# Rounds of two matmuls instead of four in the decay products of 16 gated heads, with keys and queries of both token blocks gathered by ScalarE

## The chip, the core and the metric

The kernel runs on one core of a Trainium2 chip. The time is what the device takes for one execution, in microseconds (us). PE is TensorE (PEld its weight loads), ACT is ScalarE, DVE is VectorE, POOL is GpSimd, SP issues DMAs. A bank is one of the eight accumulators that PE writes and ACT or DVE read.

## The reference, cut to what matters

Two transformer layers' worth of blocks run on 256 tokens of width 2048: a gated MLP, a hybrid mixer (dilated attention and gated linear attention), a cross attention over 256 memory tokens, a second MLP, then a recurrent block (RG-LRU and a gated recurrence with 16 heads) and a differential attention. The change is about the 16 heads:

```python
def hgrn2_chunkwise(q, k, v, log_f):
    ...
    def step(state, inp):
        qc, kc, vc, gc = inp
        b = jnp.cumsum(gc, axis=2)
        o_inter = jnp.einsum('bhtk,bhkv->bhtv', qc * jnp.exp(b), state)
        decay = jnp.exp(jnp.where(mask, b[:, :, :, None, :] - b[:, :, None, :, :], -jnp.inf))
        scores = jnp.einsum('bhtk,bhsk,bhtsk->bhts', qc, kc, decay)
        o = o_inter + jnp.einsum('bhts,bhsv->bhtv', scores, vc)
    ...
```

For each head (128 keys, 128 values) the score of query t and key s is their product times a decay by the product of all forget gates between them. The kernel computes the whole lower triangle of the 256 x 256 scores, without chunks and without a state.

## The kernel before

**Weights.** The kernel is a row of stages by name: up1a to dn1c (first MLP), mixa, gla, wout, memk, xq, memv, xo (cross attention), up2a to dn2c, rg, rouA, hg, rouB, att, aout. Every stage streams weights in units of 512 KB, one at a time through a ring of RING = 4 slots: SP loads `w_raw`, ACT rounds it to `w_high` (L1053), DVE makes the rest `w_low` (L1533), PE multiplies both (L553 to L556, or L593 to L595 for token-major units of 12 matmuls). ACT and DVE run LEAD = 3 units ahead of PE. A split waits until PE has finished the unit that used its slot.

**Banks.** A unit accumulates in one of the two banks of `gemm`; DVE takes a bank out (L1565, L2085) before PE may start it again (`evacuated`, L554).

**hg.** Eight iterations (`each`, `heads_phase`) of 16 units, with two heads in each. The table `AT_H` says at which unit of the iteration which step of the heads stands, on all engines alike: `(step, 0)` belongs to this iteration's heads, `(step, 1)` to those of the iteration before. PE does a step ahead of the unit with that number.

**Decay products.** The scores come by levels. At level s a token range of 2^s tokens is a half: queries in an odd half meet keys in the even half to their left. Tiles: `B` holds the keys of both heads (`B[:, 2:4, :]`, 256 tokens), `C` the queries, `Dm` the gates; all three are parts of `work`. PE (`decay`, L784) multiplies keys and queries of each token block of 128 (2 heads x 2 blocks = 4 matmuls of 128 x 128) into a bank (`p_a` and `p_b` in turn). DVE (L1817) copies from it what the mask of this level picks (`level_masks`) into `scores_t` (`ST[:, head, 0 or 1 or 2, :]`: 0 and 2 the two diagonal blocks, 1 the block between them). POOL (L2284, L2295, L2296, L2299) scales the odd queries and the even keys by the gates' products of the level for the next round. Step 0 needs no gate; step 7 is the last within a block (L781, 64 x 64), step 8 the block between the two (L772). Semaphores: PE's `round` lets POOL scale and DVE copy; POOL's `started` (first product) lets round 1 go, its `updated` the later rounds; DVE's `placed` gives a bank back. "mix" (L747, L748) multiplies the scores with the values, "oturn" (L754) transposes.

**rouA1** takes its banks by `lead` (two of them) and **memv** runs the cross attention's steps inside its eight units: PE scores (L931) at unit 2, DVE `largest`, ACT `power` (L1363), DVE `weigh` (L1986), PE `turn` (L943), ACT `copy_probs` (L1369), two heads at a time at units 2 to 6, then L990 multiplies with the values (L2031).

## Time and profile before

| | us |
|---|---|
| time, median of 3 runs | 3301.19 (3300.79 to 3301.6) |
| the profiled execution | 3301.96 |
| its span in the profile | 3300.2 |
| PE busy | 3267.8 (99%) |
| DVE busy | 2222.7 (67%) |
| ACT busy | 1720.4 (52%) |
| POOL busy | 367.3 (11%) |

The profile is of one execution. Busy times are sums over an engine's rows. In a timeline each row is one group of like instructions that follow one another: start, duration, line, what it writes and reads, how many; in brackets the idle time of the engine ahead of it and whose work ended that. A matmul in full float32 leaves two records, so that four matmuls are a row of x8. A matmul row's duration holds the drain of its last matmul, over which the next work already runs: what a row costs is the distance to the next one.

### The profile page before, as it was taken

What the parts mean: (1) busy time and instruction counts of PE and PEld (TensorE: products, weight loads), DVE (VectorE), ACT (ScalarE), POOL (GpSimd) and SP (SyncE); (2) the same over time, 40 slices, a digit from 0 to 9 for tenths busy, and PEclk for the clock granted to TensorE, in tenths of its full rate; (3) what the DMA queues carried; (4) which work ended last, traced back from release to release, by engine and by line L of the source; (5) the groups of instructions that cost most, each with busy time, mean ns of one, the idle gap of its engine ahead of it and who ended that gap; (6) DMA issues with size and microseconds to landing.
All of it is one profiled execution on the core that took longest, in us unless ns stands there. A gap on an engine that the chain in (4) does not pass through costs nothing.

```text
span 3300.2 us, 54641 instructions
## 1 busy us (share of the span) xinstructions
PE 3267.8 (99%) x17950; PEld 2811.3 (85%) x17950; DVE 2222.7 (67%) x3262; ACT 1720.4 (52%) x2555; POOL 367.3 (11%) x378
## 2 busy tenths in 40 slices
PE   8999999999999999999999999999999999999999
PEld 7888888887888878888888888888888888888888
DVE  7666666677655867666676677887556567666566
ACT  5444444455555655444444456764444445555554
POOL 1000000011000301000000001220333341100000
PEclk9999999999999999999999999999999999999999
DMA  6666566555555655656666656556555555555555
GB/s 228 188 198 186 186 193 186 188 180 165 172 170 175 200 156 176 190 188 185 192 186 186 190 177 198 184 173 187 158 153 159 154 157 173 185 169 180 172 172 165
DMA packets 280057, 592.46 MB, mean 180 GB/s; under 512 B 19856, under 2 KB 171664, under 8 KB 279840
## 3 DMA queue, kind: packets, MB, share of 16 engines
q1 hardware_dynamic: 278816, 587.12, 57.1%
q10 hardware_dynamic: 1152, 4.19, 0.3%
q8 instruction: 51, 0.84, 0.1%
q14 instruction: 38, 0.31, 0.0%
HBM read 589.14 MB, written 2.10 MB: 179 GB/s over the span
## 4 chain that ended last, share of the span: by engine, by line
PE 90%; issue 4%; DVE 4%; ACT 1%; POOL 0%; DMA 0%; SPq 0%; POOLq 0%; ACTq 0%; DVEq 0%
PE bank L554 41%; PE bank L553 10%; PE bank L556 10%; PE bank L593 7%; PE bank L595 7%; PE bank L594 7%; PE bank L784 2%; DVE w_low L1533 2%; PE bank L796 1%; DVE normed L1578 1%; ACT w_high L1053 1%; POOL work L2296 0%; PE bank L748 0%; PE bank L678 0%; DMA w_raw<-w_up1a 0%
## 5 line engine op out<-in xcount | busy, mean ns | idle before, releaser
L1533 DVE TENSOR_TENSOR w_low<-w_raw,w_high 128x1024 fp32r<-128x1024 f32 (+1 forms) x1120 | 1374.5, 1236 | 637.9 <-ACT w_high L1053 619.1
L1053 ACT ACTIVATE w_high<-w_raw 128x1024 fp32r<-128x1024 f32 (+1 forms) x1120 | 1166.4, 1044 | 765.0 <-PE bank L595 408.5
L554 PE MATMUL bank<-normed,w_high 128*128 128x512 f32 x3968 | 1263.4, 397 | 12.0 <-DVE w_low L1533 9.9
L554 PE MATMUL bank<-mixed,w_high 128*128 128x512 f32 x2432 | 771.3, 397 | 5.2 <-DVE increment L1565 4.3
L554 PEld LDWEIGHTS bank<-normed,w_high 128*128 128x128 f32 x3968 | 609.7, 189 | 13.6 <-issue 9.9
L553 PE MATMUL bank<-normed,w_low 128*128 128x256 f32 x1984 | 552.8, 279 | 0.0
L556 PE MATMUL bank<-normed,w_low 128*128 128x256 f32 x1984 | 550.9, 278 | 0.0
L593 PE MATMUL bank<-w_high,normed 128*128 128x512 f32 x1152 | 462.9, 402 | 1.1 <-DVE w_low L1533 1.1
L553 PEld LDWEIGHTS bank<-normed,w_low 128*128 128x128 f32 x1984 | 373.0, 188 | 90.8
L595 PE MATMUL bank<-w_high,normed 128*128 128x512 f32 x1152 | 450.0, 391 | 0.0
L594 PE MATMUL bank<-w_low,normed 128*128 128x512 f32 x1152 | 449.3, 390 | 0.0
L556 PEld LDWEIGHTS bank<-normed,w_low 128*128 128x128 f32 x1984 | 373.7, 188 | 83.8
L1073 ACT ACTIVATE parts<-bank 128x256 f32<-128x256 f32 x376 | 144.5, 384 | 575.5 <-PE bank L554 575.3
L554 PEld LDWEIGHTS bank<-mixed,w_high 128*128 128x128 f32 x2432 | 373.0, 189 | 7.5 <-DVE w_low L1533 3.8
L553 PE MATMUL bank<-mixed,w_low 128*128 128x256 f32 x1216 | 338.9, 279 | 0.0
L556 PE MATMUL bank<-mixed,w_low 128*128 128x256 f32 x1216 | 337.6, 278 | 0.0
L553 PEld LDWEIGHTS bank<-mixed,w_low 128*128 128x128 f32 x1216 | 228.6, 188 | 55.6
L556 PEld LDWEIGHTS bank<-mixed,w_low 128*128 128x128 f32 x1216 | 229.0, 188 | 51.8
L595 PEld LDWEIGHTS bank<-w_high,normed 128*128 128x128 f32 x1152 | 216.5, 188 | 46.4
L593 PEld LDWEIGHTS bank<-w_high,normed 128*128 128x128 f32 x1152 | 217.0, 188 | 42.9 <-issue 1.7
L594 PEld LDWEIGHTS bank<-w_low,normed 128*128 128x128 f32 x1152 | 217.1, 188 | 41.9
L1556 DVE TENSOR_TENSOR increment<-bank,parts 128x256 f32<-128x256 f32 x244 | 103.5, 424 | 214.9 <-ACT parts L1073 214.9
(312 smaller groups left out, 2275.5 us busy)
## 6 DMA issues: line engine op xcount, KB each, us to landing
w_raw<-w_att SPq DMA_DIRECT2D x128, 512.0 KB, 3.9
w_raw<-w_up1a SPq DMA_DIRECT2D x64, 512.0 KB, 4.2
w_raw<-w_up1b SPq DMA_DIRECT2D x64, 512.0 KB, 4.1
w_raw<-w_up2a SPq DMA_DIRECT2D x64, 512.0 KB, 4.1
w_raw<-w_up2b SPq DMA_DIRECT2D x64, 512.0 KB, 3.9
w_raw<-w_rg SPq DMA_DIRECT2D x64, 512.0 KB, 4.2
w_raw<-w_hg SPq DMA_DIRECT2D x64, 512.0 KB, 3.6
w_raw<-w_hg SPq DMA_DIRECT2D x128, 256.0 KB, 2.8
```

What stands on the lines that cost most here:

```text
L553: nc.tensor.matmul(banks[b][:, 0:S], lo, x[:, 0:S], start=False, stop=False)
L554: last = nc.tensor.matmul(banks[b][:, :], hi, x, start=starts and k == 0, stop=stop)
L556: last = nc.tensor.matmul(banks[b][:, 0:S], lo, x[:, 0:S], start=False, stop=False)
L593: nc.tensor.matmul(banks[b][:, :], x_hi, hi, start=starts and k == 0, stop=False)
L594: nc.tensor.matmul(banks[b][:, :], x_hi, lo, start=False, stop=False)
L595: last = nc.tensor.matmul(banks[b][:, :], x_lo, hi, start=False, stop=stops and k == UT // 4 - 1)
L784: last = nc.tensor.matmul(b_out[:, c * P:(c + 1) * P], B[:, 2 + hd, b * P:(b + 1) * P], rhs[:, hd, b * P:(b + 1) * P], start=True, stop=True)
L796: last = nc.tensor.matmul(b_out[:, n * S:(n + 1) * S], gw[:, t * P:(t + 1) * P], C[:, k, :], start=k == 0, stop=k == 1)
L1053: A_(wh[slot][:, 0:width], raw[slot][:, 0:width], ACT.Copy).then_inc(wh_done, 1)
L1073: A_(parts[b], banks[b][:, S:2 * S], ACT.Copy).then_inc(part_ready, 1)
L1533: TT(wl[slot][:, 0:width], raw[slot][:, 0:width], wh[slot][:, 0:width].bitcast(F32), ALU.subtract).then_inc(wl_done, 1)
L1556: TT(inc[:, b, :], gemm[b][:, 0:S], part[b], ALU.add).then_inc(evacuated, 1)
```

## The change

- In hg, rounds 1 to 7 have two matmuls, one for each head (L801 after). Their weights are the new tile `held` (a part of `gate_weights`): in each place the keys of token block 0 in even halves, the queries of block 1 in odd halves. Their moving side is `passed`: the keys of block 1 and the queries of block 0 read in place in `work`. One product then holds block 0's scores as keys by queries, and block 1's as queries by keys.
- ACT fills `held` ahead of each of these rounds with two copies (L1246, L1247), which wait for POOL's `started` or `updated`. PE waits for ACT's new `held`.
- DVE picks with two masked copies of 128 x 2 x 64, and block 1's scores land the other way round. The new step 9 (at unit 2 of the next iteration) transposes them: two PE transposes (L786) and one DVE copy to `turned`. The mix waits for that.
- The masks for the other orientation are made once, in up2b (six PE transposes) between DVE copies in dn2a and dn2b; POOL clears a part of `scores_t` at the start of rg.
- POOL's products and their order in hg stay as they are.
- rouA1 uses four banks in turn. In memv DVE's `largest` and ACT's `power` stand for all four heads at unit 2, `weigh` for all at unit 3; `turn` and `copy_probs` of heads 0 and 1 at unit 5, of heads 2 and 3 behind the last unit. In up1a ACT's four partial sums of squares move from units 0 to 2 to units 1 to 4, one each.

Line numbers of the changed kernel are higher than before: L784 is L801 or L813, L593 to L595 are L609 to L611, L1053 is L1093.

ACT in hg, units 8 to 15 of one iteration: from the last preparation of the gates over the splits beside rounds 1 to 5. `mixed` is the store of the heads before.

```order
L1232 ACTIVATE work<-work 128x512
...
L1053 ACTIVATE w_high<-w_raw 128x1024
...
L1217 ACTIVATE mixed<-bank,vectors 128x2x256
...
L1053 ACTIVATE w_high<-w_raw 128x1024
...
L1053 ACTIVATE w_high<-w_raw 128x1024 x2
...
L1053 ACTIVATE w_high<-w_raw 128x1024
```

```order
L1093 ACTIVATE w_high<-w_raw 128x1024
...
L1268 ACTIVATE mixed<-bank,vectors 128x2x256
...
L1093 ACTIVATE w_high<-w_raw 128x1024
...
L1246 ACTIVATE gate_weights<-work 128x2x64
L1247 ACTIVATE gate_weights<-work 128x2x64
...
L1246 ACTIVATE gate_weights<-work 128x2x32x2
L1247 ACTIVATE gate_weights<-work 128x2x32x2
...
L1093 ACTIVATE w_high<-w_raw 128x1024
...
L1246 ACTIVATE gate_weights<-work 128x2x16x4
L1247 ACTIVATE gate_weights<-work 128x2x16x4
```

In the first piece ACT has nothing but splits beside the rounds. In the second a pair of copies stands ahead of each round, two pairs (for rounds 1 and 2) behind the split of unit 13, and the next splits behind the pairs.

PE in hg, around rounds 0 to 2. `work` are keys and queries, `normed` the tokens of the unit.

```order
L595 MATMUL bank<-w_high,normed 128x512
...
L784 MATMUL bank<-work 128x128 x8
...
L593 MATMUL bank<-w_high,normed 128x512
L594 MATMUL bank<-w_low,normed 128x512
...
L595 MATMUL bank<-w_high,normed 128x512
...
L784 MATMUL bank<-work 128x128 x4
```

```order
L611 MATMUL bank<-w_high,normed 128x512
...
L813 MATMUL bank<-work 128x128 x4
...
L801 MATMUL bank<-work,gate_weights 128x128 x2
...
L609 MATMUL bank<-w_high,normed 128x512
L610 MATMUL bank<-w_low,normed 128x512
...
L611 MATMUL bank<-w_high,normed 128x512
...
L801 MATMUL bank<-work,gate_weights 128x128 x2
```

Before, rounds 0 and 1 are one piece of eight matmuls. After, round 1 has its own wait (for ACT's copies, `gate_weights`) right behind round 0, ahead of the unit.

ACT in memv, from the splits behind the gains of the cross attention's queries on: L1363 and L1414 are the exponentials, L1369 and L1420 the copies of the turned probabilities.

```order
L1053 ACTIVATE w_high<-w_raw 128x1024 x2
L1363 ACT_TABLE_LOAD
L1363 ACTIVATE work,softmax_stats<-bank,softmax_stats,q_rstd 128x256 x4
L1053 ACTIVATE w_high<-w_raw 128x1024
L1363 ACTIVATE work,softmax_stats<-bank,softmax_stats,q_rstd 128x256 x4
L1053 ACTIVATE w_high<-w_raw 128x1024
L1369 ACTIVATE gate_weights<-bank 128x512 x2
L1053 ACTIVATE w_high<-w_raw 128x1024
L1369 ACTIVATE block_products<-bank 128x512
L1369 ACTIVATE probs_t<-bank 128x512
L1053 ACTIVATE w_high<-w_raw 128x1024
L1412 ACTIVATE mem_values<-bank,mem_rstd 128x4x128
```

```order
L1093 ACTIVATE w_high<-w_raw 128x1024
L1414 ACT_TABLE_LOAD
L1414 ACTIVATE work,softmax_stats<-bank,softmax_stats,q_rstd 128x256 x8
L1093 ACTIVATE w_high<-w_raw 128x1024 x3
L1420 ACTIVATE gate_weights<-bank 128x512 x2
L1093 ACTIVATE w_high<-w_raw 128x1024 x2
L1463 ACTIVATE mem_values<-bank,mem_rstd 128x4x128
L1420 ACTIVATE block_products<-bank 128x512
L1420 ACTIVATE probs_t<-bank 128x512
```

All eight exponentials now stand together ahead of three splits, and the copies of heads 2 and 3 (`block_products`, `probs_t`) behind the last split and the values.

```diff
                 10: [("oturn", 1)], 11: [("store", 1), (0, 0)]}
-        AT_H = {0: [("values", 1), (7, 1)], 1: [(8, 1)], 3: [("mix", 1)], 4: [("norm", 1)], 5: [("gate", 1)], 7: [("oturn", 1)],
+        AT_H = {0: [("values", 1), (7, 1)], 1: [(8, 1)], 2: [(9, 1)], 3: [("mix", 1)], 4: [("norm", 1)], 5: [("gate", 1)], 7: [("oturn", 1)],
                 8: [("prepare", 0)], 9: [("store", 1)], 10: [(0, 0), (1, 0)]}
...
+            if name == "rouA1" and j // 2 % 2:
+                return p_t, p_o
             return (p_b, p_o) if name == "aout1" and j < 2 else gemm
...
             return (it - HEADS_G) * 16 + (place["hg"][0] * RING + 16)
+
+        def pieces(offset, step, h):
+
+            pair = work[:, :, :].rearrange("p n s -> p (n s)")[:, offset:offset + 2 * (step + h)]
+            return pair.rearrange("p (e r) -> p e r", e=2)[:, :, 0:P].rearrange("p e (n u t) -> p e n u t", u=2, t=h)[:, :, :, 0, :]
+
+        def passed(hd, step):
+
+            return pieces((6 + hd) * S + P, S + P, 1 << (step - 1))
...
         def _(pe):
-            def unit(qq, slot, parts, src, banks=gemm, later=None):
+            def unit(qq, slot, parts, src, banks=gemm, later=None, depth=2):
...
                 for b, k0, nk, starts, stops, grp in parts:
-                    if starts and not (isinstance(grp, int) and grp < len(banks)):
-
-                        pe.wait_ge(evacuated, grp - (len(banks) - 1))
+                    if starts and not (isinstance(grp, int) and grp < depth):
+
+                        pe.wait_ge(evacuated, grp - (depth - 1))
                     for k in range(nk):
...
                 if step == "mix":
-                    pe.wait_ge(dec["placed"], rounds(it, heads) + (3 if heads == 1 else 9))
+                    pe.wait_ge(dec["placed"], rounds(it, heads) + (3 if heads == 1 else 10))
                     pe.wait_ge(rec["valued"], it + 1)
...
                             nc.tensor.matmul(to, ST[:, n, 1, :], V_D[:, 0, cols], start=True, stop=False)
-                        last = nc.tensor.matmul(to, ST[:, n, 2 * b, :], V_D[:, b, cols], start=b == 0, stop=True)
+                        own_block = ST[:, n, 2 * b, :] if heads == 1 else turned[:, n, :] if b else ST[:, n, 2, :]
+                        last = nc.tensor.matmul(to, own_block, V_D[:, b, cols], start=b == 0, stop=True)
                     last.then_inc(rec["mixed"], 1)
...
                         pe.wait_ge(dec["placed"], rounds(it, 1) + (step - 6))
+                    if step == 9:
+                        pe.wait_ge(dec["placed"], rounds(it, 2) + 8)
+                        for hd in range(2):
+                            last = nc.tensor.transpose(b_out[:, hd * P:(hd + 1) * P], ST[:, hd, 0, :], C_("ident"))
+                        last.then_inc(dec["round"], 1)
+                        return
+                    if heads == 2 and 1 <= step <= 7:
+                        pe.wait_ge(dec["held"], keeps(it) + step)
                     if heads == 2 and step >= 2:
...
                             continue
-                        rhs = B if step == 0 and heads == 2 else C
+                        if heads == 2 and step:
+                            last = nc.tensor.matmul(b_out[:, hd * P:(hd + 1) * P], held[:, hd, :], passed(hd, step),
+                                                    start=True, stop=True)
+                            continue
+                        rhs = B if heads == 2 else C
                         for b in range(NB):
-                            c = 2 * hd + b
+                            c = 2 * hd + (b if heads == 1 else 1 - b)
                             if step == LEVELS - 1:
...
                             score(hd)
-                    if j in (5, 6):
-                        turn(2 * j - 10)
-                        turn(2 * j - 9)
+                    if j == 5:
+                        turn(0)
+                        turn(1)
                     unit_tokens(q0 + j // RING, j % RING, 2 * j, XN, mem_banks, j == 0, j == 7)
+                turn(2)
+                turn(3)
                 pe.wait_ge(mem["valued"], 2)
...
             for name in names:
+                if name == "up2b":
+                    pe.wait_ge(dec["spread"], 1)
+                    flat = C[:, :, :].rearrange("p n s -> p (n s)")
+                    for step in range(6):
+                        last = nc.tensor.transpose((p_a, p_b)[step // 4][:, step % 4 * P:(step % 4 + 1) * P],
+                                                   flat[:, step * P:(step + 1) * P], C_("ident"))
+                    last.then_inc(dec["faced"], 1)
                 if name.startswith("up"):
...
                     prepare(it, grp, heads, it)
+                if heads == 2 and isinstance(step, int) and step < 7:
+                    h = 1 << step
+                    if step == 0:
+                        act.wait_ge(dec["started"], it + 1)
+                    else:
+                        act.wait_ge(dec["updated"], updates(it, 2) + step)
+                    to = held.rearrange("p h (n u t) -> p h n u t", u=2, t=h)
+                    keys = B[:, 2:4, 0:P].rearrange("p h (n u t) -> p h n u t", u=2, t=h)
+                    queries = C[:, 0:2, P:S].rearrange("p h (n u t) -> p h n u t", u=2, t=h)
+                    A_(to[:, :, :, 0, :], keys[:, :, :, 0, :], ACT.Copy)
+                    A_(to[:, :, :, 1, :], queries[:, :, :, 1, :], ACT.Copy).then_inc(dec["held"], 1)
                 if step == "values":
...
                                scale=cross_gain[:, 0:1]).then_inc(crs["gained"], 1)
-                    if j in (3, 4):
-                        power(2 * j - 6)
-                        power(2 * j - 5)
-                    if j in (5, 6):
-                        copy_probs(2 * j - 10)
-                        copy_probs(2 * j - 9)
+                    if j == 2:
+                        for hd in range(HEADS_X):
+                            power(hd)
+                    if j == 5:
+                        copy_probs(0)
+                        copy_probs(1)
                 act.wait_ge(pe_unit, place["xo"][0] * RING)
...
                    scale=rstd_m[:, 1:2]).then_inc(mem["valued"], 1)
+                copy_probs(2)
+                copy_probs(3)
                 for hd in range(HEADS_X):
...
                         dve.wait_ge(dec["placed"], rounds(it, heads) + at)
+                    if heads == 2 and step == 0:
+                        dve.wait_ge(dec["cleared"], 1)
                     if not isinstance(it, int):
...
                             "p (h s) -> p h s", h=heads)).then_inc(dec["placed"], 1)
+                    elif step == 9:
+                        nc.vector.tensor_copy(turned, b_in[:, 0:2 * P].rearrange(
+                            "p (h s) -> p h s", h=2)).then_inc(dec["placed"], 1)
+                    elif step == LEVELS - 1 and heads == 2:
+                        x = b_in[:, 0:2 * P].rearrange("p (h e t) -> p h e t", h=2, e=2)
+                        nc.vector.tensor_copy(ST[P // 2:P, :, 0, 0:P // 2], x[P // 2:P, :, 0, :])
+                        nc.vector.tensor_copy(ST[0:P // 2, :, 2, P // 2:P], x[0:P // 2, :, 1, :]).then_inc(dec["placed"], 1)
+                    elif heads == 2 and step:
+                        h = 1 << (step - 1)
+                        x = b_in[:, 0:2 * P].rearrange("p (h e n t) -> p h e n t", h=2, e=2, t=h)
+                        for e in range(2):
+                            last = nc.vector.copy_predicated(
+                                ST[:, :, 2 * e, :].rearrange("p h (n u t) -> p h n u t", u=2, t=h)[:, :, :, e, :],
+                                level_mask[:, step, :].rearrange("p (n u t) -> p n u t", u=2, t=h)[:, :, e, :].unsqueeze(1
+                                ).broadcast_to([P, 2, P // (2 * h), h]),
+                                x[:, :, e, :, :])
+                        last.then_inc(dec["placed"], 1)
                     elif step == LEVELS - 1:
...
                     if j in (2, 3):
-                        largest(2 * j - 4)
-                        largest(2 * j - 3)
-                    if j in (4, 5):
-                        weigh(2 * j - 8)
-                        weigh(2 * j - 7)
+                        for hd in range(HEADS_X):
+                            (largest, weigh)[j - 2](hd)
                 dve.wait_ge(rms["rooted"], NORMED["memk"] + 1)
...
                 PT_(C[:, 0:heads, :], B[:, 0:heads, :], Dm[:, 0:heads, :], ALU.mult).then_inc(dec["started"], 1)
-                total, at = Dm[:, 0:heads, :].rearrange("p h s -> p (h s)"), 0
+                total, at = Dm[:, 0:2, :].rearrange("p h s -> p (h s)"), 0
                 for level in range(LEVELS - 1):
                     half = 1 << level
-                    n = heads * S // (2 * half)
-                    qv = C[:, 0:heads, :].rearrange("p h (n e t) -> p (h n) e t", e=2, t=half)
-                    kv = B[:, 2:2 + heads, :].rearrange("p h (n e t) -> p (h n) e t", e=2, t=half)
+                    n = S // half
+                    all_q = C[:, 0:2, :].rearrange("p h (n e t) -> p (h n) e t", e=2, t=half)
+                    all_k = B[:, 2:4, :].rearrange("p h (n e t) -> p (h n) e t", e=2, t=half)
                     tv = total.rearrange("p (n e) -> p n e", e=2)
-
-                    pool.wait_ge(dec["round"], rounds(it, heads) + (level + 2))
-                    own.settle()
-                    PT_(qv[:, :, 1, :], qv[:, :, 1, :], tv[:, :, 0:1].broadcast_to([P, n, half]), ALU.mult)
-                    PT_(kv[:, :, 0, :], kv[:, :, 0, :], tv[:, :, 1:2].broadcast_to([P, n, half]),
+                    pool.wait_ge(dec["round"], rounds(it, 2) + (level + 2))
+                    own.settle()
+                    PT_(all_q[:, :, 1, :], all_q[:, :, 1, :], tv[:, :, 0:1].broadcast_to([P, n, half]), ALU.mult)
+                    PT_(all_k[:, :, 0, :], all_k[:, :, 0, :], tv[:, :, 1:2].broadcast_to([P, n, half]),
                         ALU.mult).then_inc(dec["updated"], 1)
```

## Rows read from the trace of the kernel before

**Rows 1.** The page, part 1: busy us, share and instructions of each engine

```profile
PE 3267.8 (99%) x17950; PEld 2811.3 (85%) x17950; DVE 2222.7 (67%) x3262; ACT 1720.4 (52%) x2555; POOL 367.3 (11%) x378
```

**Rows 2.** PE's waits: line, what it waited for, us in total, times, longest

```profile
PE bank L554 <- DVE increment L1565: 4.3, 6, 1.8
...
PE bank L554 <- DVE work L2085: 1.4, 1, 1.4
...
PE bank L990 <- DVE mem_values L2031: 0.9, 1, 0.9
```

**Rows 3.** Busy time by stretch: us, PE, PEld, DVE, ACT, POOL, PEclk, DMA

```profile
2308.00:2740.00 432.00, 430.06 (x2458) 368.55 (x2457) 261.07 (x367) 202.17 (x298) 158.38 (x175) 1.00 0.50 156
1200.00:1220.00 20.00, 17.69 (x76) 14.42 (x76) 12.93 (x27) 12.14 (x26) 1.64 (x1) 0.92 0.38 118
2226.00:2230.00 4.00, 3.99 (x16) 3.48 (x17) 3.36 (x5) 0.00 (x0) 0.00 (x0) 0.64 0.23 88
25.00:29.00 4.00, 3.82 (x22) 3.36 (x23) 4.00 (x4) 1.16 (x2) 3.78 (x3) 1.00 0.82 256
```

**Rows 4.** Timeline of PE, one iteration: start, us, line, operation, [idle before]

```profile
2434.02 1.95 PE L784 MATMUL bank<-work 128*128 128x128 f32 x16
...
2438.91 1.15 PE L784 MATMUL bank<-work 128*128 128x128 f32 x8 [0.19 <-POOL work L2296]
...
2446.30 1.06 PE L784 MATMUL bank<-work 128*128 128x128 f32 x8
...
2449.94 1.05 PE L784 MATMUL bank<-work 128*128 128x128 f32 x8
...
2457.33 0.68 PE L781 MATMUL bank<-work 128*64 128x64 f32 x8
...
2460.83 0.60 PE L772 MATMUL bank<-work 128*128 128x128 f32 x4
...
2466.85 0.60 PE L748 MATMUL bank<-v_raw_and_tokens,scores_t 128*128 128x128 f32 x4
...
2479.34 0.60 PE L754 MATMUL bank<-constants,head_out 128*128 128x128 f32 x4
```

**Rows 5.** Timeline of POOL, the same iteration

```profile
2433.43 1.29 POOL L2284 TENSOR_TENSOR work<-work 128x512 f32<-128x512 f32 x1 [12.41 <-ACT work L1232]
...
2440.22 1.46 POOL L2295 TENSOR_TENSOR work<-work,block_products 128x256 f32<-128x256 f32 x1 [0.86 <-PE bank L784]
2441.64 0.75 POOL L2296 TENSOR_TENSOR work<-work,block_products 128x256 f32<-128x256 f32 x1
...
2447.53 0.65 POOL L2295 TENSOR_TENSOR work<-work,block_products 128x256 f32<-128x256 f32 x1 [1.12 <-PE bank L784]
2448.13 1.63 POOL L2296 TENSOR_TENSOR work<-work,block_products 128x256 f32<-128x256 f32 x1
```

**Rows 6.** ACT: timeline in gla and hg, and the group of L1149

```profile
933.06 0.40 ACT L1234 ACTIVATE work<-work 128x256 f32<-128x256 f32 x1
933.37 0.40 ACT L1235 ACTIVATE work<-work 128x256 f32<-128x256 f32 x1
...
2434.78 1.05 ACT L1053 ACTIVATE w_high<-w_raw 128x1024 fp32r<-128x1024 f32 x1
...
L1149 ACT ACTIVATE work<-work,root_qk 128x128 f32<-128x128 f32 x48 | 16.0, 389 | 3.9 <-POOL root_qk L2251 3.9
```

**Rows 7.** Timeline of DVE, the same iteration

```profile
2439.84 1.23 DVE L1533 TENSOR_TENSOR w_low<-w_raw,w_high 128x1024 fp32r<-128x1024 f32 x1 [0.16 <-ACT w_high L1053]
...
2447.59 1.66 DVE L1533 TENSOR_TENSOR w_low<-w_raw,w_high 128x1024 fp32r<-128x1024 f32 x1 [1.28 <-ACT w_high L1053]
...
2465.71 1.22 DVE L1533 TENSOR_TENSOR w_low<-w_raw,w_high 128x1024 fp32r<-128x1024 f32 x1
```

**Rows 8.** Timeline of PE in memv and in rouA1

```profile
1216.49 1.84 PE L943 MATMUL bank<-constants,work 128*128 128x128 f32 x8 [2.31 <-DVE work L1986]
...
2226.01 0.47 PE L554 MATMUL bank<-mixed,w_high 128*128 128x512 f32 x1 [1.81 <-DVE increment L1565]
```

31 lines of the change are left out of this document (25 added, 6 removed).

## The prediction

> **What bounds the kernel now.** I read the page's busy line first: PE is busy for 3267.8 of 3300.2 us [rows 1]. So the time is PE's work plus some 32 us in which PE waits, and an edit counts only if it changes PE's own instructions, or a wait of PE. The view of PE's waits names those [rows 2]: the longest is for the first split at the start, which the change does not touch; the others are small and single, and rows 2 keeps the three that the change aims at. The table by stage comes next [rows 3]: the decay phase (2308 to 2740 us, eight iterations of 54 us, all of it at full clock) has PE busy for 430.06 of 432.00 us. There is nothing to win there from waits, only from PE instructions, and much to lose if a new wait appears. The rounds of one iteration in the timelines of PE and POOL [rows 4, 5] show how close that is. PE starts a round at 2446.30 and the next at 2449.94, 3.65 us later: 2.74 us of unit work (12 matmuls 0.23 us apart, as they follow one another in PE's timeline) and 0.90 us for the round. Beside it runs a chain: the round ends (2447.36), POOL starts 0.17 us later (2447.53) and ends at 2449.76, and PE's next round starts at 2449.94. The chain is 0.1 to 0.2 us shorter than PE's own period. PE bounds the rounds, by a hair, and POOL is next.
>
> **The sum is made against the profiled run, 3301.96 us** (span 3300.2), 0.77 us above the median of 3301.19; I take that off at the end.
>
> **The rounds.** A round of steps 1 to 6 has four matmuls before and two after. Half of 0.90 is 0.45 for two matmuls of this size. Such two stand in the trace as step 8 (a row of 4 records, 0.60 us long, of which the last matmul's drain lies under the next work) [rows 4]. So a round costs PE 0.45 us less, and PE alone would have a period of 3.20 us. But the chain gains a link: POOL's products, then two ACT copies, then PE. Each copy has 128 elements a partition. No such copy stands in the trace. The 256-wide copies are 0.40 us each, the second starting 0.31 after the first, the 1024-wide split 1.057 [rows 6]. The slope between them, 0.85 ns an element, gives 0.29 for one and 0.50 us for the pair. The nearest 128-wide row is L1149 with 389 ns, which has a scale per row; two of those are 0.69. I take 0.50, because the copies have no scale, and keep 0.69 for the range. The two new hand-overs I take as 0.04 (POOL to ACT) and 0.10 us (ACT to PE), estimates below the 0.17 that PE to POOL takes in this round; at 0.17 each the chain would be 0.2 longer.
>
> The chain after: round 0.60 (the row of 4 records) + 0.17 + POOL 2.23 (2447.53 to 2449.76) + 0.04 + 0.50 + 0.10 = **3.64 us**. It replaces PE's 3.65. What PE saves in a round is what it then waits: about 0.45 us idle before each round. The term that can move is POOL's 2.23. Alone its two products are 0.65 and 0.75; the other 0.8 is DVE's split, which stretches whichever product it meets (L2296 1.63 us at 2448.13 while the DVE split is 1.66; L2295 1.46 us at 2440.22) [rows 5, 7]. DVE's split follows ACT's split, which follows the end of the unit ahead of the round. If PE idles 0.45 us before the round, the split comes 0.45 earlier against the round, at +0.85 instead of +1.29, and POOL starts at +0.77. That is on the edge. If the split wins, both products stand behind it: at 2440.22 the level ended 1.32 us after the split's end. A level is then at most 1.23 + 1.32 = 2.55. I take 3.70 for the period, between 3.64 and 3.96.
>
> **Round 1** is where time is lost for certain. Rounds 0 and 1 stand back to back before (the x16 row at 2434.02, round 1 at about 2434.93). Now round 1 needs the copies, which need POOL's first product (2433.43 + 1.29 = 2434.72), and on ACT's queue they stand behind the split of 2434.78, which ends at 2435.83 [rows 5, 6]. Copies until 2436.33, round 1 at about 2436.4: PE idles some 1.4 us. It saves 0.47 of that by two matmuls less. Then POOL starts at 2437.15 with DVE's split already running, as at 2440.22, where the level took 2.17; with the split further on than there it takes 1.8 to 2.1 and ends at about 2439.1. With 0.64 for copies and hand-overs round 2 starts at 2439.7 where it was 2438.91: +0.8. Behind the waiting copies on ACT stands the next split. It starts 0.8 us later than now, and since PE uses a split three units later (8 us), nobody waits for it.
>
> Rounds 2 to 7: five periods of 3.70 for 18.42 us before, +0.1. Step 7 was four small matmuls for some 0.6 us (the row of 0.68) and is two for 0.45: -0.15. The new step 9 has two transposes at 0.11 (four at 2479.34, 0.60 with the drain, 0.44 without): +0.22 [rows 4]. Its copy on DVE stands behind a split that ends at 2466.93 [rows 7] and takes about 0.42, with the mix at 2466.85 now waiting for it; both shift together by 0.9, so PE waits some 0.4 us there. Sum: 0.8 + 0.1 - 0.15 + 0.22 + 0.4 = **+1.4 us an iteration, +11 for eight**. With the chain at 3.64, a level as short after round 1 as the first figure says and no wait at the mix it is +0.5, so +4; with 3.85 it is +2.3, so +19.
>
> DVE's mask copies get shorter and are on no path. POOL's memset and the masks' copies in dn2a and dn2b stand beside PE work in stages where PE waits for nothing, with splits three units ahead, 8 us: nothing. The six transposes in up2b are PE work: 6 x 0.11 = +0.7.
>
> **The other waits.** rouA1: DVE's take of an accumulated bank comes late behind the scan and PE stands for 1.81 us at 2226.01 [rows 8]; with four banks it need not wait. After the stop the granted clock is 0.64 over the next 4 us [rows 3]: most of that stretch ran at 1.2 GHz and not 2.4, and 4 x 0.36 = 1.4 us were lost. With 0.4 us of the other waits on this take (six make 4.3 [rows 2]), -3.6. memv: PE stands 2.31 us for the weighing at 1216.49 [rows 8]; the weighing moves from units 4 and 5 to unit 3 and the exponentials to unit 2. The eight of L1363 are 4.4 us in a row on ACT and the splits behind them come later, but the turns are needed only at unit 5, 8.2 us on. The clock is 0.92 in those 20 us: 1.6 us more. Also 0.9 us for the values (L990) [rows 2], which two moved turns now cover. Together -4.8. If the later splits make PE wait instead, -3. Start: PE waits 1.4 us (L554 on DVE's L2085) [rows 2] for a take that stands behind two DVE splits; the squares move off ACT's way and the splits come about one ACT operation earlier: -1.4, between -0.5 and -1.6. Sum of the side edits: -3.6 - 4.8 - 1.4 + 0.7 = **-9.1**, between -6 and -11.
>
> **Total**: 3301.96 + 11.2 - 9.1 = 3304.1, minus 0.77: **3303 us**. No change that a measurement can tell: some 0.2% (6.6 us) is what it can.
>
> **The rivals.**
> A, PE bounds the rounds. If the DVE split fell outside POOL's two products, a level would be 1.40 and the chain 2.81, and the period would be PE's 3.20. An iteration gets 0.8 - 5 x 0.49 - 0.15 + 0.22 + 0.4 = -1.2 us, eight -10, total 3301.2 - 10 - 9.1 = 3282. Against it: PE, ACT and DVE follow one another so that the split starts at +0.85 to +1.29 and POOL works from +0.77 to +2.2; every level in the trace meets it. Chance 0.12.
> B, slower: the clock falls. PE idles about 1.4 us ahead of round 1, eight times. It fell after idle times of 1.81 and 2.31 us [rows 8]; it did not after the 1.4 at the start [rows 2], where the clock is 1.00 over the next 4 us [rows 3]. It decides from somewhere between these. Then each iteration loses up to 1.6 us, less the 0.45 of one round's slack: 8 x 1.2 = +10, total 3313. Chance 0.13.
> C, slower: the chain is longer than priced, by the split going ahead of POOL (2.55), the pair at 0.69 and 0.15 to PE: up to 0.60 + 0.17 + 2.55 + 0.04 + 0.69 + 0.15 = 4.20. Every 0.1 us above 3.65 costs 5 x 8 x 0.1 = 4 us; at 3.95 it is +12 over my sum with 1 more at round 2, total 3315; at 4.20 3325. It decides from 3.85 on (by which the total passes 3308). For it: POOL's 1.46 us product, which shows that order [rows 5]. Against: only then is PE idle long enough that the split leads, and the two orders hold each other near 3.75. Chance 0.13.
> The Trainium skill ("SBUF — State Buffer", section "Who interferes with whom") says that issue order decides who blocks: the engine that comes first to the shared pair holds it for the whole instruction. By that rule the product behind the split of 2447.59 to 2449.25 would need its whole 0.75 us after it; the row ends 0.51 after. By the rule the chain would be 3.88 and the time about 3310, near rival C; by the row it is 3.64, and the trace decides.
> D, the side edits do not give what I took (another wait takes the place of the one removed, as the splits behind eight exponentials would in memv): -6 instead of -9.1, 3306. It lies in my forecast's range.
>
> **Chances.** Forecast with D 0.62, A 0.12, B 0.13, C 0.13. The range 3290 to 3315 leaves out A (0.12) and half of C and a tail of B, together about 0.2. Faster by over 0.2% (below 3294.6): A and the lowest part of the forecast, 0.18. Slower (above 3307.8): B, C and the forecast's upper end, 0.3. Same: 0.52.
>
> **What the profile after would show.** PE rows of two matmuls, about 0.44 of PE time each, 3.7 us apart, each with an idle of 0.4 to 0.5 before it, released by ACT; ahead of round 1 an idle of 1.2 to 1.5. Some 33 to 38 us of new PE waits on the copies in all (8 x (1.4 + 6 x 0.45 + 0.4) = 36). POOL products of 2.2 us in sum a level. ACT pairs of 0.5. No PE wait over 1 us in rouA1 and memv and the clock at 1.00 there. Window 2308 to 2740 grown by some 11 us. I am wrong if the period is 3.2 or above 3.85, if the clock drops in the decay phase, or if an iteration waits elsewhere.

## The result and the profile after

| | before | after |
|---|---|---|
| time, median of 8 runs, us | 3301.97 | 3312.59 |
| span of the profiled execution, us | 3300.2 | 3310.5 |
| PE busy, us | 3267.8 | 3256.6 |

The changed kernel is slower: the ratio is 1.0033, with a 95% interval of 1.0024 to 1.0043. One of its eight executions took 3402.81 us at a granted clock of 0.916, and the ratio leaves it out. The forecast was 3303 us, in a range of 3290 to 3315.

The page, part 1, of the changed kernel (compare [rows 1]), and under it its PE waits (compare [rows 2]):

```profile
PE 3256.6 (98%) x17748; PEld 2788.6 (84%) x17748; DVE 2206.1 (67%) x3285; ACT 1745.5 (53%) x2667; POOL 363.9 (11%) x379
```

```profile
PE bank L801 <- ACT gate_weights L1247: 27.1, 53, 1.2
PE bank L570 <- DVE w_low L1586: 12.1, 2, 10.2
PE bank L570 <- DVE increment L1618: 2.1, 4, 1.1
...
PE bank L765 <- DVE gate_weights L1866: 1.1, 7, 0.2
```

PE has 11 us less work and 22 us more idle time. One new wait, for ACT's copies, makes 27.1 us (53 times), and some of the old ones are gone. The waits of [rows 2] for L1565 have gone from 4.3 to 2.1 us, those for L2085 and for the values (L990) are gone, and so is the one of [rows 8] in memv.

Where the 10.3 us come from can be read off landmarks: PE instructions that wait for the same thing in both kernels, and so mark the same point of the program. First of the kernel before, then of the changed one (PE timeline; start, duration, line, idle before):

```profile
40.62 0.70 PE L643 MATMUL bank<-diag,ones 128*128 128x256 f32 x2 [0.36 <-DVE diag L1652]
...
1198.69 1.06 PE L950 MATMUL bank<-constants,work 128*128 128x128 f32 x8 [0.44 <-DVE work L2020]
...
1264.13 0.61 PE L622 MATMUL bank<-ones,squares_sum 128*128 128x1 f32 x4 [0.28 <-DVE normed L1578]
...
1715.21 0.50 PE L554 MATMUL bank<-mixed,w_high 128*128 128x512 f32 x1 [0.86 <-DVE w_low L1533]
...
2325.60 1.16 PE L784 MATMUL bank<-work 128*128 128x128 f32 x8 [0.38 <-ACT work L1232]
```

```profile
39.46 0.70 PE L659 MATMUL bank<-diag,ones 128*128 128x256 f32 x2 [0.38 <-DVE diag L1705]
...
1197.53 1.07 PE L980 MATMUL bank<-constants,work 128*128 128x128 f32 x8 [0.44 <-DVE work L2092]
...
1257.86 0.61 PE L638 MATMUL bank<-ones,squares_sum 128*128 128x1 f32 x4 [0.27 <-DVE normed L1631]
...
1710.62 0.50 PE L570 MATMUL bank<-mixed,w_high 128*128 128x512 f32 x1 [1.88 <-DVE w_low L1586]
...
2316.61 1.16 PE L813 MATMUL bank<-work 128*128 128x128 f32 x8 [0.38 <-ACT work L1283]
```

The differences after minus before are -1.16 us at the first two (the start), -6.27 at the third, -4.59 at the fourth and -8.99 at round 0 of hg. So the start gave 1.2 us, memv 5.1, and rouA1 4.4; between the third and the fourth, where the masks are turned, 1.7 were lost. The start is the least certain of these: its landmark lies between 38.09 and 39.46 us in the profiles of the changed kernel and of the experiments below that have its new start, and at 40.62 and 40.96 in the two with the old one, so that the gain there is 1.2 to 2.9 us by the execution. In that place stood:

```profile
1708.31 0.87 DVE L2214 CAST level_masks<-bank 128x64 int32<-128x64 f32 x6
1709.34 3.50 DVE L1586 TENSOR_TENSOR w_low<-w_raw,w_high 128x1024 fp32r<-128x1024 f32 x3 [0.16 <-DVE level_masks L2214]
```

Six casts of the turned masks stand ahead of three queued splits on DVE, 1.03 us from the first cast to the splits, and PE's wait at the fourth landmark is 1.88 instead of 0.86.

The granted clock is full again where it was 0.92 and 0.64 in [rows 3] (windows of the changed kernel, columns as there):

```profile
1200.00:1220.00 20.00, 20.00 (x94) 16.78 (x94) 13.27 (x28) 12.61 (x26) 1.64 (x1) 1.00 0.37 128
2226.00:2240.00 14.00, 14.00 (x83) 12.22 (x82) 11.77 (x19) 6.68 (x10) 0.00 (x0) 1.00 0.75 234
```

So 9.0 us are won ahead of hg, and all of it and 9.7 more are lost in it (0.6 more behind it). One iteration of the changed kernel (PE timeline, compare [rows 4]):

```profile
2428.56 1.06 PE L813 MATMUL bank<-work 128*128 128x128 f32 x8
2430.82 0.72 PE L801 MATMUL bank<-work,gate_weights 128*128 128x128 f32 x4 [1.21 <-ACT gate_weights L1247]
...
2434.43 0.72 PE L801 MATMUL bank<-work,gate_weights 128*128 128x128 f32 x4 [0.15 <-issue]
...
2438.54 0.71 PE L801 MATMUL bank<-work,gate_weights 128*128 128x128 f32 x4 [0.64 <-ACT gate_weights L1247]
...
2446.32 0.71 PE L801 MATMUL bank<-work,gate_weights 128*128 128x128 f32 x4 [0.42 <-ACT gate_weights L1247]
...
2450.12 0.71 PE L801 MATMUL bank<-work,gate_weights 128*128 128x128 f32 x4 [0.34 <-ACT gate_weights L1247]
...
2453.96 0.71 PE L801 MATMUL bank<-work,gate_weights 128*128 128x128 f32 x4 [0.37 <-ACT gate_weights L1247]
...
2463.87 0.71 PE L765 MATMUL bank<-v_raw_and_tokens,scores_t 128*128 128x128 f32 x4 [0.15 <-DVE gate_weights L1866]
```

Measured from round 0 (2434.02 before, 2428.56 after), round 2 is at 5.87 us instead of 4.89, round 7 at 25.40 instead of 23.31, and the mix at 35.31 instead of 32.83. An iteration is 56.6 us instead of 54.0. What sets the period shows beside the rounds of 2446.32 and 2450.12 on POOL, ACT and DVE (compare [rows 5, 6, 7]):

```profile
2447.19 1.58 POOL L2376 TENSOR_TENSOR work<-work,block_products 128x256 f32<-128x256 f32 x1 [1.46 <-PE bank L801]
2448.72 0.63 POOL L2377 TENSOR_TENSOR work<-work,block_products 128x256 f32<-128x256 f32 x1
```

```profile
2449.39 0.31 ACT L1246 ACTIVATE gate_weights<-work 128x128 f32<-128x128 f32 x1 [2.38 <-POOL work L2377]
2449.61 0.29 ACT L1247 ACTIVATE gate_weights<-work 128x128 f32<-128x128 f32 x1
```

```profile
2447.05 1.23 DVE L1586 TENSOR_TENSOR w_low<-w_raw,w_high 128x1024 fp32r<-128x1024 f32 x1 [2.23 <-ACT w_high L1093]
```

The chain reads: round 0.71, to POOL 0.16, POOL 2.16 (2447.19 to 2449.35), to ACT 0.04, the pair 0.51 (2449.39 to 2449.90), to PE 0.22. That is 3.80 us, the distance of the two rounds. DVE's split now starts 0.14 us ahead of POOL, and POOL's first product is the long one (1.58), not the second as in [rows 5].

The 4.11 us between the rounds of 2434.43 and 2438.54 have the same links but a longer one on POOL:

```profile
2435.32 0.74 POOL L2376 TENSOR_TENSOR work<-work,block_products 128x256 f32<-128x256 f32 x1 [1.10 <-PE bank L801]
2436.02 1.73 POOL L2377 TENSOR_TENSOR work<-work,block_products 128x256 f32<-128x256 f32 x1
```

That level takes 2.43 us (2435.32 to 2437.75). POOL was first there, by 0.09 us, and the product that met nothing took 0.74 and not 0.63. The four levels after it take 2.26, 2.22, 2.16 and 2.20.

PE's idle times understate what the chain costs. Where nothing makes PE wait its rounds come 3.19 us apart (dve_after_pool below), so it stands for some 0.6 us of these 3.80, of which the profile counts 0.34 as idle: the drain of the matmul ahead of the wait and the longer round behind it count as busy.

### The profile page after: what moved, and what is told of

It reads as the page before. It is cut to its first block, busy times and chain, and to the rows that moved or that the text cites. A ratio compares the mean times of both kernels' runs of the same rounds, so it can differ in the third digit from the quotient of the medians.

```text
span 3310.5 us, 54497 instructions
## 1 busy us (share of the span) xinstructions
PE 3256.6 (98%) x17748; PEld 2788.6 (84%) x17748; DVE 2206.1 (67%) x3285; ACT 1745.5 (53%) x2667; POOL 363.9 (11%) x379
## 4 chain that ended last, share of the span: by engine, by line
PE 87%; issue 4%; DVE 4%; ACT 3%; POOL 2%; DMA 0%; ACTq 0%; POOLq 0%; SPq 0%; DVEq 0%
PE bank L570 43%; PE bank L569 11%; PE bank L572 11%; PE bank L609 6%; PE bank L611 6%; PE bank L610 6%; ACT w_high L1093 1%; DVE w_low L1586 1%; PE bank L801 1%; POOL work L2377 1%; PE bank L825 1%; DVE normed L1631 1%; ACT gate_weights L1247 0%; PE bank L765 0%; PE bank L694 0%
## 5 line engine op out<-in xcount | busy, mean ns | idle before, releaser
L1093 ACT ACTIVATE w_high<-w_raw 128x1024 fp32r<-128x1024 f32 (+1 forms) x1120 | 1166.0, 1044 | 630.9 <-PE bank L570 347.8
L570 PE MATMUL bank<-normed,w_high 128*128 128x512 f32 x3968 | 1265.0, 397 | 10.9 <-DVE w_low L1586 10.2
L570 PEld LDWEIGHTS bank<-normed,w_high 128*128 128x128 f32 x3968 | 610.3, 189 | 11.7 <-issue 10.2
L609 PE MATMUL bank<-w_high,normed 128*128 128x512 f32 x1152 | 462.4, 401 | 1.1 <-DVE w_low L1586 1.1
L611 PE MATMUL bank<-w_high,normed 128*128 128x512 f32 x1152 | 449.7, 390 | 0.0
L611 PEld LDWEIGHTS bank<-w_high,normed 128*128 128x128 f32 x1152 | 216.2, 188 | 46.4
L609 PEld LDWEIGHTS bank<-w_high,normed 128*128 128x128 f32 x1152 | 216.6, 188 | 42.9 <-issue 1.7
```

The costliest lines, as they stand in the source:

```text
L570: last = nc.tensor.matmul(banks[b][:, :], hi, x, start=starts and k == 0, stop=stop)
L609: nc.tensor.matmul(banks[b][:, :], x_hi, hi, start=starts and k == 0, stop=False)
L611: last = nc.tensor.matmul(banks[b][:, :], x_lo, hi, start=False, stop=stops and k == UT // 4 - 1)
L1093: A_(wh[slot][:, 0:width], raw[slot][:, 0:width], ACT.Copy).then_inc(wh_done, 1)
```

## The experiments

The twelve kernels ran in three groups of four, each beside the kernel before, whose median was 3301.34 (sides_only, decay_only, dve_after_pool, copy_more), 3301.8 (held_wait_last, first_pair_early, dve_after_pool_from_2, from_2_and_pair) and 3302.77 us (the other four). Ratios are to it. Where a difference is between kernels of different groups, or to the changed kernel with its 3312.59 us, it is uncertain by this 1 to 1.5 us. Line numbers shift by a few between the kernels.

Two things ahead of hg differ from profile to profile and have nothing to do with the edits in it: the start, as said, and whether the clock falls behind a wait of 1.9 us in dn2a (see the masks below; 1.8 us). The time from round 0 of hg's first iteration to the end of the span is free of both; it can still hold up to some 2 us of slow clock in the last 40 us:

| kernel | us |
|---|---|
| before | 974.6 |
| changed | 993.9 |
| sides_only | 974.9 |
| decay_only | 993.5 |
| dve_after_pool | 977.6 |
| dve_after_pool_from_2 | 966.1 |
| old_rounds_dve_after_pool | 974.5 |
| copy_more | 1003.3 |
| held_wait_last | 987.0 |
| first_pair_early | 992.2 |
| from_2_and_pair | 964.9 |
| split_between | 956.0 |
| masks_later | 993.6 |
| split_between_masks_later | 956.3 |

**The parts alone.** The edit of the first is to leave the decay part out, of the second to leave the edits of rouA1, memv and up1a out; the diff of both is a part of the one shown with the change.

> The kernel before with the edits outside the decay products alone: four banks in rouA1, the moved steps of memv, the moved squares of up1a; no mirrored masks, rounds of four matmuls. My theory (the side edits and the decay part add up, each read off the trace by the shift of landmarks): -1.2 at the start, -5.1 in memv, -4.4 in rouA1, so 10.7 us less than the kernel before, 3291 us. A rival by which the gains were only shifted waits that come back later in the kernel: less than 6 us gained, 3296 or more.

Measured: 3291.16 us, ratio 0.9968 (0.9956 to 0.998): -10.2.

> The changed kernel with those three side edits undone: rounds of two matmuls, the masks mirrored in dn2a to dn2b, step 9. Theory: the decay phase costs +18.7 and the masks +1.7 by the landmarks of the two traces, so 21 us above the kernel before, 3323 us. If the slower decay phase and the faster side edits were tied to one another (the phase starts 9 us earlier in the changed kernel), it would be off that by 3 us or more.

Measured: 3322.18 us, ratio 1.0062 (1.0048 to 1.0076): +20.8. The two add up to +10.6, which is what the change does. Within the noise the parts are independent, and the landmarks told their sizes (-10.7 and +21 expected).

**POOL and DVE apart.** DVE waits ahead of its split until POOL's products of the level are done:

```diff
+                        if name == "hg" and 10 <= j <= 15:
+                            dve.wait_ge(dec["updated"], updates(i + HEADS_G, 2) + (j - 9))
+                            if not isinstance(i, int):
+                                dve.sem_inc(dve_passed, 1)
                         ahead(name, qq, j, nb, last)
```

> The changed kernel; DVE's split beside each of rounds 1 to 6 waits until POOL's two products of that level are done (one wait more on DVE, nothing else). Theory: what makes the period 3.85 us is the meeting of POOL's products with DVE's split; apart, a level is 1.35 us, the chain 3.0, and PE bounds the rounds at 3.20 to 3.25 us. Five periods 0.6 shorter and round 2 0.4 earlier, 8 iterations: 27 us less than the changed kernel, 3285 us, with POOL's products at 0.65 and 0.65. Rival 1: the two copies on ACT and their hand-overs bound the period by themselves; then the products get shorter but the period stays above 3.6, 3305 or more. Rival 2: the splits now come too late for PE and waits on w_low take the gain: over 3 us of such waits in the decay phase.

Measured: 3296.22 us, ratio 0.9983 (0.9974 to 0.9992): 16 us less than the changed kernel, where 27 were expected. Its PE timeline in one iteration, then POOL beside the round of 2440.05, and DVE:

```profile
2433.53 0.72 PE L801 MATMUL bank<-work,gate_weights 128*128 128x128 f32 x4 [1.57 <-DVE scores_t L1889]
...
2436.84 0.61 PE L801 MATMUL bank<-work,gate_weights 128*128 128x128 f32 x4
...
2440.05 0.61 PE L801 MATMUL bank<-work,gate_weights 128*128 128x128 f32 x4
```

```profile
2440.82 0.65 POOL L2380 TENSOR_TENSOR work<-work,block_products 128x256 f32<-128x256 f32 x1 [1.65 <-PE bank L801]
2441.43 0.65 POOL L2381 TENSOR_TENSOR work<-work,block_products 128x256 f32<-128x256 f32 x1
```

```profile
2432.64 0.76 DVE L1889 COPY_PREDICATED scores_t<-level_masks,bank 128x256 f32<-128x256 int32 x2
...
2442.32 1.23 DVE L1586 TENSOR_TENSOR w_low<-w_raw,w_high 128x1024 fp32r<-128x1024 f32 x1 [1.54 <-POOL work L2381]
```

POOL's products are 0.65 each and rounds 3 to 7 come 3.19 to 3.21 us apart with no idle time: PE bounds them. Rival 1 falls, and no wait on w_low appeared, so rival 2 falls too. The missing 11 us are at round 2, where PE waits 1.57 us for DVE's masked copy of round 0 (2432.64), which stands behind the split that now waits: seven such waits, 10.9 us in all.

Without the wait beside round 1:

```diff
-                        if name == "hg" and 10 <= j <= 15:
+                        if name == "hg" and 11 <= j <= 15:
```

> As dve_after_pool, without the wait at round 1 (so beside rounds 2 to 6 only). There rounds 3 to 7 came 3.19 us apart, but round 2 waited 1.57 us for DVE's masked copies of round 0, which stood behind the delayed split. Theory: round 2 is where the changed kernel has it and the five periods are 3.2: 8 x 3.6 = 29 us less than the changed kernel, 3284 us. If the delayed splits cost something of their own, it is over 3288.

Measured: 3284.62 us, ratio 0.9947 (0.9934 to 0.9961), 28 us less than the changed kernel, where the theory had 29.

**The old rounds with the same wait.** The same edit on the kernel of sides_only:

> The kernel of sides_only (rounds of four matmuls) with the wait of dve_after_pool_from_2 on DVE. Theory: there PE itself bounds the rounds at 3.65 us, so shorter POOL levels give nothing but the 0.1 us before round 2 that they never had: within 1.5 us of sides_only, 3291. Rival: the old rounds were bound by the same meeting of POOL and DVE; then they gain as the new ones did, 10 us or more.

Measured: 3290.44 us, ratio 0.9962 (0.9948 to 0.9976). The median is 0.7 us below that of sides_only, but its group ran 1.4 us slower; from round 0 of hg to the end the two differ by 0.4 us. POOL beside the round of 2434.90 in it:

```profile
2436.12 0.65 POOL L2303 TENSOR_TENSOR work<-work,block_products 128x256 f32<-128x256 f32 x1 [2.09 <-PE bank L786]
2436.73 0.65 POOL L2304 TENSOR_TENSOR work<-work,block_products 128x256 f32<-128x256 f32 x1
```

The level is 1.26 us, one microsecond shorter than the 2.24 in sides_only, and the rounds come 3.65 us apart all the same. So the old rounds are bound by PE, and the rival falls: with four matmuls the chain is shorter by ACT's link and PE's own period longer, and the meeting of POOL and DVE costs nothing. Only with the change does it come onto the path.

**The link on ACT.** One copy more ahead of each pair:

```diff
+                    spare = FD[:, 2:4, P:S].rearrange("p h (n u t) -> p h n u t", u=2, t=h)
+                    A_(spare[:, :, :, 0, :], keys[:, :, :, 0, :], ACT.Copy)
                     A_(to[:, :, :, 0, :], keys[:, :, :, 0, :], ACT.Copy)
```

> The changed kernel with one copy more on ACT (the same keys once more, into a part of the tile that nothing reads, 0.21 us to the next) ahead of each pair. Theory: POOL, ACT's pair, PE's round are one loop with nothing beside it that gives; +0.2 us for each of seven rounds, eight iterations: +12 us on the changed kernel, 3324. Rival: the meeting with DVE's split sets the period, and a later round lets the split get further ahead of POOL, so that POOL's level shrinks by what ACT adds: +4 us or less, 3316.

Measured: 3322.27 us, ratio 1.0063 (1.0049 to 1.0077): +9.7 on the changed kernel (+9.4 from round 0 of hg on), nearer the theory's 12 than the rival's 4. Rounds 3 to 7 come 4.0 to 4.1 us apart. The link is on the path for four fifths of its length.

**The order of PE's waits.** In rounds 2 to 7 of the changed kernel PE waits for ACT's `held` first, then for `placed` and `updated`. The edit puts `held` last:

```diff
-                    if heads == 2 and 1 <= step <= 7:
-                        pe.wait_ge(dec["held"], keeps(it) + step)
                     if heads == 2 and step >= 2:

                         pe.wait_ge(dec["placed"], rounds(it, 2) + (step - 1))
                         pe.wait_ge(dec["updated"], updates(it, 2) + (step - 1))
+                    if heads == 2 and 1 <= step <= 7:
+                        pe.wait_ge(dec["held"], keeps(it) + step)
```

> The changed kernel; PE waits for ACT's copies behind its other two waits of the round, not ahead of them. In the changed kernel PE starts 0.05 us after the copies where it has this wait alone (round 1) and 0.22 us after them where two more, long fulfilled, stand behind it (rounds 2 to 7). Theory 1: those two cost 0.17 us on the path; without them 6 x 8 x 0.12 to 0.17, 6 to 8 us less, 3305. Theory 2: POOL's first product waits for the end of DVE's split anyway in rounds 3 to 7, whenever the round ends, so that an earlier round gains nothing in most of them: 2 us less or nothing, 3311.

Measured: 3305.86 us, ratio 1.0011 (1.0002 to 1.002), 6.7 us less than the changed kernel (6.9 from round 0 of hg on): theory 1. One round of it on PE, ACT, POOL and DVE:

```profile
2445.32 0.71 PE L801 MATMUL bank<-work,gate_weights 128*128 128x128 f32 x4 [0.24 <-ACT gate_weights L1247]
```

```profile
2444.97 0.29 ACT L1247 ACTIVATE gate_weights<-work 128x128 f32<-128x128 f32 x1
```

```profile
2446.19 0.64 POOL L2376 TENSOR_TENSOR work<-work,block_products 128x256 f32<-128x256 f32 x1 [1.27 <-PE bank L801]
2446.78 1.62 POOL L2377 TENSOR_TENSOR work<-work,block_products 128x256 f32<-128x256 f32 x1
```

```profile
2446.24 1.67 DVE L1586 TENSOR_TENSOR w_low<-w_raw,w_high 128x1024 fp32r<-128x1024 f32 x1 [1.62 <-ACT w_high L1093]
```

ACT's second copy ends at 2445.26 and PE starts at 2445.32, 0.06 us later and not 0.22. The Trainium skill ("Advanced Engine Details and Errata", section "Network/Comms") gives 50 to 100 ns for reading a semaphore's value from a sequencer; the 0.17 us for two fulfilled waits agree with that. POOL now starts 0.05 us ahead of DVE and the long product is the second again, the level 2.21 instead of 2.16: who comes first changes which product is stretched, and hardly the level.

**Round 1.** On ACT the pair for round 1 ahead of the split of its unit:

```diff
+                        if name == "hg" and j == 10:
+                            run(0, i, 0)
                         ahead(name, qq, j, nb, last)
...
-                        schedule(table, n, j, i, lambda s_, h: run(s_, h, mine + min(j, FEATURES[name]) // 2))
+                        schedule({10: [(1, 0)]} if name == "hg" and j == 10 else table, n, j, i, lambda s_, h: run(s_, h, mine + min(j, FEATURES[name]) // 2))
```

> The changed kernel; on ACT the pair of copies for round 1 stands ahead of the split of its unit, not behind it. Theory: round 1 starts 0.95 us earlier in every iteration, DVE's split of that unit comes later and meets POOL's next level, so that about half of it reaches round 2: 4 us less, up to 7; 3306 to 3308. Rival: round 2 then waits for DVE's masked copies behind the later split, and nothing is gained.

Measured: 3310.97 us, ratio 1.0029 (1.0018 to 1.004), 1.6 us less than the changed kernel (1.7 from round 0 of hg on), where the theory had 4. PE's rounds 1 and 2 and POOL between them:

```profile
2429.80 0.73 PE L801 MATMUL bank<-work,gate_weights 128*128 128x128 f32 x4 [0.27 <-ACT gate_weights L1247]
...
2434.13 0.72 PE L801 MATMUL bank<-work,gate_weights 128*128 128x128 f32 x4 [0.88 <-ACT gate_weights L1247]
```

```profile
2431.51 1.83 POOL L2379 TENSOR_TENSOR work<-work 128x256 f32<-128x256 f32 x1
```

Round 1 waits 0.27 us instead of 1.21, and round 2 then 0.88 instead of 0.15: POOL's second product takes 1.83 us instead of 0.85, since it now meets the split that moved behind the pair. The gain is given back one round later.

This edit and the wait on DVE beside rounds 2 to 6 together:

> Both of these: DVE's splits behind POOL's products beside rounds 2 to 6, and the pair of round 1 ahead of its split. Theory: the gains add up, since one moves round 1 and 2 and the other the periods behind them: 3284 - 4 = 3280, faster than every kernel so far. Rival: the first two rounds only wait elsewhere, 3284.

Measured: 3283.96 us, ratio 0.9946 (0.9932 to 0.9959), 0.7 us less than without the pair. Here the rival held: rounds 1 and 2 only trade their waits. POOL and DVE still meet between them, which the next kernel takes away.

**All of it.** PE's wait last, the first pair early, DVE's splits behind POOL beside rounds 1 to 6, and DVE's masked copy of round 0 ahead of its waiting split. PE's and ACT's parts are those above; DVE's is this, and its table of steps leaves the copy out at its old place:

```diff
+                        if name == "hg" and j == 10:
+                            run(0, i)
+                        if name == "hg" and 10 <= j <= 15:
+                            dve.wait_ge(dec["updated"], updates(i + HEADS_G, 2) + (j - 9))
+                            if not isinstance(i, int):
+                                dve.sem_inc(dve_passed, 1)
                         ahead(name, qq, j, nb, last)
```

> The changed kernel with all three: PE's wait for the copies last, ACT's first pair ahead of its split, and DVE's splits behind POOL's products beside all rounds 1 to 6, with DVE's masked copy of round 0 ahead of the split there (so that round 2 doesn't wait for it, as it did in dve_after_pool). In first_pair_early round 1 came 0.95 us earlier but POOL's product met the split moved behind the pair (1.83 us instead of 0.85), so nothing reached round 2. Theory: with them apart round 2 starts when unit 10 ends, 3.2 us behind round 1, 1.1 us earlier than in from_2_and_pair: 8 to 9 us less than that, 3275 us. Rival: nothing is left to win there (PE waits for something else at round 2), 3284.

Measured: 3274.95 us, ratio 0.9916 (0.9902 to 0.9929): 27.8 us less than the kernel before in the same runs, and some 38 less than the changed one. Its rounds 1 to 3, and its wait for the copies:

```profile
2422.82 0.72 PE L801 MATMUL bank<-work,gate_weights 128*128 128x128 f32 x4 [0.27 <-ACT gate_weights L1247]
...
2426.11 0.64 PE L801 MATMUL bank<-work,gate_weights 128*128 128x128 f32 x4
...
2429.33 0.61 PE L801 MATMUL bank<-work,gate_weights 128*128 128x128 f32 x4
```

```profile
PE bank L801 <- ACT gate_weights L1247: 2.7, 8, 0.8
```

Rounds 2 and 3 have no idle time ahead of them; 2.7 us of waits on the copies are left of 27.1.

**The masks.** DVE's copy of the masks behind the adds of dn2a, not ahead of them:

```diff
-                if name == "dn2a":
-                    flat = C[:, :, :].rearrange("p n s -> p (n s)")
-                    nc.vector.tensor_copy(flat[:, 0:6 * P].rearrange("p (l s) -> p l s", l=6),
-                                          level_mask[:, 1:7, :]).then_inc(dec["spread"], 1)
...
                     add_phase(name, 0.5)
+                if name == "dn2a":
+                    flat = C[:, :, :].rearrange("p n s -> p (n s)")
+                    nc.vector.tensor_copy(flat[:, 0:6 * P].rearrange("p (l s) -> p l s", l=6),
+                                          level_mask[:, 1:7, :]).then_inc(dec["spread"], 1)
```

> The changed kernel; DVE's copy of the masks (128 x 768) stands behind the adds of dn2a, not ahead of them. The landmarks put 1.7 us on the masks: 0.7 for six transposes and 1.0 by which PE's wait on w_low at the start of dn2a is longer (0.86 to 1.88). Theory: DVE's copy delays the first splits of that stage; moved, the wait is 0.86 again: 1 us less, 3311.5, and the wait shows it. Rival: PE's wait has another cause and stays at 1.9.

Measured: 3316.86 us (four executions), ratio 1.0043 (1.0028 to 1.0059), some 4 us more than the changed kernel. The theory falls. PE's waits in those stages, and the windows of 8 us around the second, first of this kernel, then of the changed one, then of split_between, where the masks' copy is not moved:

```profile
1522.12 0.88 PE L1042 MATMUL bank<-constants,work 128*128 128x128 f32 x6 [2.07 <-DVE work L2217]
...
1711.59 0.50 PE L570 MATMUL bank<-mixed,w_high 128*128 128x512 f32 x1 [1.87 <-DVE w_low L1586]
```

```profile
1708.00:1716.00 8.00, 6.13 (x26) 5.07 (x25) 7.37 (x20) 1.41 (x3) 0.00 (x0) 0.79 0.34 108
```

```profile
1708.00:1716.00 8.00, 6.12 (x36) 5.09 (x35) 7.74 (x18) 2.78 (x4) 0.00 (x0) 1.00 0.50 163
```

```profile
1708.00:1716.00 8.00, 6.12 (x26) 5.26 (x26) 6.87 (x14) 2.66 (x4) 0.00 (x0) 0.79 0.59 186
```

The second wait is as long as before (1.87 and 1.88), so the copy in dn2a was not its cause. The six casts ahead of it are what is left, by their place and their 1.03 us; no run took them away. The moved copy made a new wait of 2.07 us ahead of the transposes. After the second wait the clock fell (0.79 over 8 us, 1.7 to 1.8 us lost), but that is not shown to come from the moved copy: it fell in the same place in split_between and four more kernels that leave the copy where it was. The profiled execution (3314.5 us) was 2.2 us or more faster than the other three; what those lost is in no profile.

> split_between with the masks' copy moved as in masks_later. Theory: the two add up, 1 us less than split_between, 3274; the best of this study if both hold.

Measured: 3279.51 us, ratio 0.9928 (0.9914 to 0.9941), 4.6 more than split_between and not 1 less. Here the clock fell behind both waits (0.79 over 1521 to 1529, and over 1710 to 1718). split_between has the second fall too, so that the pair shows what the moved copy costs: the wait of 2.07 us and the 1.8 us of slow clock behind it.

## Why the prediction was right or wrong

The time fell into the range, but the likeliest case, no change that can be told, did not happen: the kernel is slower by 10.6 us, where 3303 would have been 1 to 2. The sign that the prediction named for its being wrong, a period above 3.85, came true.

- **The side edits.** Predicted -9.1 to the start of hg, measured -9.0. In parts: start -1.4 and -1.2; memv -4.8 and -5.1; rouA1 -3.6 and -4.4; masks +0.7 and +1.7. The term for the masks was mis-sized: the step that failed is "POOL's memset and the masks' copies in dn2a and dn2b stand beside PE work in stages where PE waits for nothing". PE did wait there, 0.86 us for a split behind DVE's small operations, and that wait was in the trace. In rouA1 the price of the slow clock was taken from the first 4 us alone, which was too little.
- **Round 1.** PE idle some 1.4 us, measured 1.21; round 2 later by 0.8, measured 0.98. Nearly right. The new waits were to be 33 to 38 us; those on the copies are 27.1 and the one at the mix 1.1. Before round 2 PE stands 0.15 us and not 0.45, before round 1 1.21 and not 1.4.
- **The period.** Predicted 3.70 (3.64 to 3.96), measured 4.11 and then 3.80 to 3.89, mean 3.91 (from 2434.43 to 2453.96). This is the step that failed, +0.2 us five times in eight iterations, 8 us. Of the six links, four were right (to POOL 0.17 and 0.16, POOL 2.23 and 2.16 to 2.26, to ACT 0.04 and 0.04, the pair 0.50 and 0.51), but for POOL's 2.43 in the first period. Two were short: the round was 0.71 and not 0.60, and ACT to PE 0.22 and not 0.10. The round I took from a row in which PE had no idle time before it. The hand-over was 0.05 at round 1, where the wait is PE's only one, and 0.22 where two more waits stand behind it on PE; held_wait_last showed that these are the 0.17. The order of the waits was in the diff, and the prediction did not read it. To the forecast of 3.64 us the two links add 0.23, and POOL's first level 0.04 in the mean.
- **Step 7, step 9 and the mix.** -0.15 and -0.15 (round 7 to step 8), then +0.62 for transposes and the wait at the mix, measured +0.54 up to the mix. 0.11 us more followed in the mix, whose first row is 0.71 instead of 0.60.
- **Sum for hg.** Predicted +11.2, measured +18.7 (0.9, then 2.6 six times, then 2.3). The upper bound was added up wrong: with a period of 3.85 the terms give +2.1 an iteration and +17, not +2.3 and +19. Another 0.6 us came after hg; nothing here settles from what.
- **Rival C** is the case that came, with another make-up. The split does lead, as it said, but a level was not longer for it (2.16 and not 2.55; the one of 2.43 had POOL first): the stretched product ends 0.49 us after the split, and the other needs 0.6. The pair is not 0.69. Its price, 4 us for every 0.1 us of chain, held: from 3.70 to 3.91 it gives 8.4 us, which makes 3311.4 of the forecast's 3303, and 3312.59 were measured. The rival counted it from 3.65, though the forecast stands on 3.70, so its 3315 and 3325 are 2 us too high.
- **Rival A** did not happen, but its mechanism is right: with the split outside the products the level is 1.26 us (2440.82 to 2442.08 in dve_after_pool, 1.40 predicted) and the rounds come at PE's own 3.19.
- **Rival B** did not happen: the clock in hg stayed at 1.00 with idle times of 1.21 and 1.25, and in dve_after_pool with seven of 1.57 beside them (1.00 over 2320 to 2740).
- **The rule of the Trainium skill** ("SBUF — State Buffer", section "Who interferes with whom"): that the order of issue decides who is held back is what the runs show (POOL ahead by 0.05, second product long; DVE ahead by 0.14, first product long). That a held product needs its whole time afterwards they don't show: the first ended 0.49 after the split where it takes 0.63 alone.
